# Where ring pieces and moving tiles start within 64 bytes of SBUF: a two-block transformer kernel on one core

## The reference, cut to what matters

```python
h  = modulate(rmsnorm(x)) ; parts = h @ w_in          # first block: gated linear attention, Fourier mix
y  = (gate_fft * (fft @ w_fourier_out) + gate_gla * (o @ w_gla_out)) @ w_out
x  = x + gt1 * y
x  = x + gt2 * (square(relu(h2 @ w_mlp_in)) @ w_mlp_out)   # 2048 -> 8192 -> 2048
u  = rms_norm(x) @ w_in_2                              # second block: 2048 -> 4352
y  = concat(mixers(u)) @ w_out_2                       # 2048 -> 2048
up = rms_norm(x) @ w_up_2                              # 2048 -> 11264, then conv and gate
x  = x + rms_norm((silu(gate) * val) @ w_down_2)       # 5632 -> 2048
```

## Time and profile before

| | us |
|---|---|
| median of 3 runs | 2663.68 (2663.1 to 2665.05) |
| the profiled execution, its own time | 2666.81 |
| its span, first to last instruction | 2665.0 |
| TensorE busy in the span | 2587.0 |
| ScalarE, VectorE busy | 1139.6, 1658.2 |
| mean granted TensorE clock | 0.986 |

### The profile page before, as it was taken

The page is one execution under the profiler, slowest core; times in us unless marked ns, Lnnn a source line. Parts: engine busy times, 40 slices in busy tenths (PEclk is TensorE's granted clock), DMA queues, the critical chain, the costliest instruction groups (busy, mean ns, idle before and its releaser), DMA issues.

```text
span 2665.0 us, 42761 instructions
## 1 busy us (share of the span) xinstructions
PE 2587.0 (97%) x19024; PEld 2417.4 (91%) x19024; DVE 1658.2 (62%) x1989; ACT 1139.6 (43%) x1293; POOL 11.2 (0%) x24
## 2 busy tenths in 40 slices
PE   6799999999998999999999999999899999999998
PEld 4478799789997999999999999899899889988996
DVE  4266566557786754555555568966667647764775
ACT  3332555534435443434434454044445435543544
POOL 0000000000000000000000000000000000000000
PEclk9899999999998999999999999999999999999999
DMA  9776555567875765555555555445355555555553
GB/s 373 303 265 238 193 202 206 175 219 283 300 292 186 285 208 188 190 188 182 186 188 190 176 178 200 145 158 189 131 190 181 199 188 190 179 201 190 190 178 121
DMA packets 77225, 547.77 MB, mean 206 GB/s; under 512 B 8849, under 2 KB 8977, under 8 KB 12273
## 3 DMA queue, kind: packets, MB, share of 16 engines
q1 hardware_dynamic: 74304, 533.53, 56.9%
q0 software_dynamic: 2448, 11.01, 1.1%
q10 hardware_dynamic: 288, 0.50, 0.1%
HBM read 539.77 MB, written 5.24 MB: 205 GB/s over the span
## 4 chain that ended last, share of the span: by engine, by line
PE 92%; DMA 3%; DVE 3%; ACT 2%; issue 1%; SPq 0%; POOL 0%; DVEq 0%; ACTq 0%
PE acc L286 22%; PE acc L284 22%; PE acc L288 22%; PE acc L304 5%; PE acc L305 5%; PE acc L306 5%; PE acc L341 4%; DMA raw<-in_w_mod 2%; PE mp L304 1%; PE mp L306 1%; PE mp L305 1%; PE mp L371 1%; DVE macc L415 1%; PE mp L1820 1%; DVE wlo L252 0%
## 5 line engine op out<-in xcount | busy, mean ns | idle before, releaser
L252 DVE TENSOR_TENSOR wlo<-raw,whi 128x1024 fp32r<-128x1024 f32 x781 | 945.1, 1223 | 733.4 <-ACT whi L242 730.8
L242 ACT ACTIVATE whi<-raw 128x1024 fp32r<-128x1024 f32 x781 | 819.8, 1058 | 1220.5 <-PE acc L288 906.0
L284 PE MATMUL acc<-hh,whi 128*128 128x256 f32 x3360 | 946.9, 282 | 13.5 <-DVE wlo L252 7.8
L286 PE MATMUL acc<-hl,whi 128*128 128x256 f32 x3360 | 939.1, 279 | 0.0
L288 PE MATMUL acc<-hh,wlo 128*128 128x256 f32 x3360 | 935.6, 278 | 0.0
L284 PEld LDWEIGHTS acc<-hh,whi 128*128 128x128 f32 x3360 | 633.1, 188 | 19.9 <-issue 13.4
L286 PEld LDWEIGHTS acc<-hl,whi 128*128 128x128 f32 x3360 | 634.6, 189 | 1.4 <-issue 1.0
L288 PEld LDWEIGHTS acc<-hh,wlo 128*128 128x128 f32 x3360 | 631.9, 188 | 0.0
L286 PE MATMUL acc<-ml,whi 128*128 128x256 f32 x1536 | 431.1, 281 | 0.0
L284 PE MATMUL acc<-mh,whi 128*128 128x256 f32 x1536 | 428.3, 279 | 1.6 <-DVE wlo L252 1.6
L288 PE MATMUL acc<-mh,wlo 128*128 128x256 f32 x1536 | 427.0, 278 | 0.0
(11 more groups left out here) (310 smaller groups left out, 2219.0 us busy)
## 6 DMA issues: line engine op xcount, KB each, us to landing
raw<-in_w_in SPq DMA_DIRECT2D x98, 1024.0 KB, 4.9
raw<-in_w_mod SPq DMA_DIRECT2D x96, 1024.0 KB, 5.4
raw<-in_w_up SPq DMA_DIRECT2D x88, 1024.0 KB, 4.9
raw<-in_w_mlp_in SPq DMA_DIRECT2D x64, 1024.0 KB, 4.9
raw<-in_w_mlp_out SPq DMA_DIRECT2D x64, 1024.0 KB, 4.9
raw<-in_w_down SPq DMA_DIRECT2D x44, 1024.0 KB, 4.9
raw<-in_w_out SPq DMA_DIRECT2D x32, 1024.0 KB, 5.0
raw<-in_w_fourier_out SPq DMA_DIRECT2D x8, 1024.0 KB, 5.2
```

Of the source, the lines that this page charges most:

```text
L242: nc.scalar.activation(whi[:, r, :], raw_slot(k)[:, 2 * GC * j:2 * GC * (j + 1)], ACT.Copy)\
L252: nc.vector.tensor_tensor(wlo[:, r, :], raw_slot(k)[:, 2 * GC * j:2 * GC * (j + 1)], whi[:, r, :].bitcast(f32), ALU.subtract).then_inc(S[" ...
L284: nc.tensor.matmul(dst, whi[:, r, cols], hi[:, kt, :], start=begin, stop=False, skip_group_check=True)
L286: nc.tensor.matmul(dst, whi[:, r, cols], lo[:, kt, :], start=False, stop=False, skip_group_check=True)
```

## The change: what it does

Each ring slot grows from 1024 to 1040 elements (4096 to 4160 bytes), and a table PLACE says for each piece how many elements behind its slot's start it begins: 0, 4 or 8, which is offset 0, 16 or 32. All users go through a new function `ring`.

- 332 pieces (w_mlp_in, w_mlp_out, w_in_2, w_out_2) go from offset 16 to 32.
- The 88 pieces of w_down_2 go from 16 to 0.
- All others stay at 16.
- The activation tiles of the MLP, w_in_2 and w_out_2 get new tensors over the same regions, 16 bytes further: `nh`/`nl` in place of `hh`/`hl`, `rh`/`rl` in place of `mh`/`ml`. Their offset goes from 32 to 48. The merge in front of w_out keeps `mh`/`ml`, and w_up_2 keeps `hh`/`hl`.
- The two rings are 192 bytes longer each and the region of `hh` 64 bytes. What lies behind moves by 192, 384 or 448 bytes, all multiples of 64.

No instruction is added, removed or reordered; no size, wait or queue changes.

```diff
+BLOCK = len(PIECE) - 588
+PLACE = [4] * len(PIECE)
+PLACE[BLOCK:BLOCK + 332] = [8] * 332
+for _end, _n in ((len(PIECE) - 168, 32), (len(PIECE) - 72, 32), (len(PIECE), 24)):
+    PLACE[_end - _n:_end] = [0] * _n
...
-        whi = sb("whi", [P, 8 * GC + 16], f32r)[:, 4:8 * GC + 4].rearrange("p (r n) -> p r n", r=4)
-        wlo = sb("wlo", [P, 8 * GC + 16], f32r)[:, 4:8 * GC + 4].rearrange("p (r n) -> p r n", r=4)
+        whi = sb("whi", [P, 4, 2 * GC + 16], f32r)
+        wlo = sb("wlo", [P, 4, 2 * GC + 16], f32r)
...
-        (hh, hl, xN, gN) = overlay(
-            "region_h", 32768,
+        (hh, hl, nhl, xN, gN) = overlay(
+            "region_h", 32768 + 64,
             [("hh", [P, KT, NT], f32r), ("hl", [P, KT, NT], f32r)],
+            [("nhl", [P, 2 * KT * NT + 16], f32r)],
...
+            [("rhl", [P, 2 * KT * NT + 16], f32r)],
...
+        halves = lambda ap: [ap[:, 4 + i * KT * NT:4 + (i + 1) * KT * NT].rearrange("p (k n) -> p k n", n=NT)
+                             for i in range(2)]
+        (nh, nl), (rh, rl) = halves(nhl), halves(rhl)
...
+        def ring(part, p):
+
+            return part[:, p % 4, PLACE[p]:PLACE[p] + 2 * GC]
...
-            nc.scalar.activation(whi[:, r, :], raw_slot(k)[:, 2 * GC * j:2 * GC * (j + 1)], ACT.Copy)\
+            nc.scalar.activation(ring(whi, st.p), raw_slot(k)[:, 2 * GC * j:2 * GC * (j + 1)], ACT.Copy)\
...
             for c in range(0, MLP_CHUNKS):
                 for g in range(4):
-                    mm_feature(pe, st, g % 2, hh, hl, 0, each=n2_ready if c + g == 0 else None,
+                    mm_feature(pe, st, g % 2, nh, nl, 0, each=n2_ready if c + g == 0 else None,
...
-                    mm_feature(pe, st, g % 2, mh, ml, 1, free=(S["rsq_ok"], 4 * c + g + 3) if g < 2 else None,
+                    mm_feature(pe, st, g % 2, rh, rl, 1, free=(S["rsq_ok"], 4 * c + g + 3) if g < 2 else None,
```

More of the change, by code:

```diff
@@ L249, in lo_piece @@
                 mod_acc(dve, st)
-            r = st.p % 4
             dve.wait_ge(S["hi_n"], st.p + 1)
-            nc.vector.tensor_tensor(wlo[:, r, :], raw_slot(k)[:, 2 * GC * j:2 * GC * (j + 1)],
-                                    whi[:, r, :].bitcast(f32), ALU.subtract).then_inc(S["lo_n"], 1)
+            nc.vector.tensor_tensor(ring(wlo, st.p), raw_slot(k)[:, 2 * GC * j:2 * GC * (j + 1)],
+                                    ring(whi, st.p).bitcast(f32), ALU.subtract).then_inc(S["lo_n"], 1)
             st.p += 1
@@ L274, in feature_piece @@
         def feature_piece(pe, st, i, hi, lo, k0, nkt=KT, w=GC):
-            r = st.p % 4
+            wh, wl = ring(whi, st.p), ring(wlo, st.p)
             pe.wait_ge(S["lo_n"], st.p + 1)
@@ L283, in feature_piece @@
                     begin = kt == 0 and t % 2 == 0
-                    nc.tensor.matmul(dst, whi[:, r, cols], hi[:, kt, :], start=begin, stop=False,
+                    nc.tensor.matmul(dst, wh[:, cols], hi[:, kt, :], start=begin, stop=False,
                                      skip_group_check=True)
-                    nc.tensor.matmul(dst, whi[:, r, cols], lo[:, kt, :], start=False, stop=False,
+                    nc.tensor.matmul(dst, wh[:, cols], lo[:, kt, :], start=False, stop=False,
                                      skip_group_check=True)
-                    last = nc.tensor.matmul(dst, wlo[:, r, cols], hi[:, kt, :], start=False,
+                    last = nc.tensor.matmul(dst, wl[:, cols], hi[:, kt, :], start=False,
                                             stop=kt == nkt - 1, skip_group_check=True)
@@ L303, in token_piece @@
                     dst = bank[:, off:off + GC]
-                    nc.tensor.matmul(dst, hi[:, kt, t0:t0 + P], whi[:, r, cols], start=kt == 0, stop=False)
-                    nc.tensor.matmul(dst, hi[:, kt, t0:t0 + P], wlo[:, r, cols], start=False, stop=False)
-                    last = nc.tensor.matmul(dst, lo[:, kt, t0:t0 + P], whi[:, r, cols], start=False,
+                    nc.tensor.matmul(dst, hi[:, kt, t0:t0 + P], wh[:, cols], start=kt == 0, stop=False)
+                    nc.tensor.matmul(dst, hi[:, kt, t0:t0 + P], wl[:, cols], start=False, stop=False)
+                    last = nc.tensor.matmul(dst, lo[:, kt, t0:t0 + P], wh[:, cols], start=False,
                                             stop=kt == nkt - 1)
@@ L355, in mm_lr @@
                     dst = acc[i][0:LRW, x * GC:x * GC + NT]
-                    nc.tensor.matmul(dst, whi[:, r, cols], hi[:, kt, :], start=kt == 0, stop=False)
-                    nc.tensor.matmul(dst, whi[:, r, cols], lo[:, kt, :], start=False, stop=False)
-                    last = nc.tensor.matmul(dst, wlo[:, r, cols], hi[:, kt, :], start=False, stop=kt == KT - 1)
+                    nc.tensor.matmul(dst, wh[:, cols], hi[:, kt, :], start=kt == 0, stop=False)
+                    nc.tensor.matmul(dst, wh[:, cols], lo[:, kt, :], start=False, stop=False)
+                    last = nc.tensor.matmul(dst, wl[:, cols], hi[:, kt, :], start=False, stop=kt == KT - 1)
             last.then_inc(S["used"], 1)
@@ L1278, in _ @@
             own(nc.vector.reciprocal(rstd[:, 0, :], root[:, :]))
-            apply_dve(dve, 8, 0, [(xT2, hh, hl, a, n) for a, n in N2_JOBS])
+            apply_dve(dve, 8, 0, [(xT2, nh, nl, a, n) for a, n in N2_JOBS])
             def mix_lo(g):
@@ L1909, in mixer_sums @@
                     last.then_inc(S["ln_ps"], 1)
[L1910 to L1912 removed]
+            mm_feature(pe, st, 0, nh, nl, 1, each=mixer_sums)
+            mm_feature(pe, st, 1, nh, nl, 1)
+            mm_feature(pe, st, 0, nh, nl, 1, w=NT)
             def mixed(s):
```

31 lines of the change are left out of this document (15 added, 16 removed).

## The result

The changed kernel is slower: 2681.8 us (median of 4, 2678.9 to 2684.4) against 2664.4, a ratio of 1.0060 with a 95% interval of 1.0046 to 1.0074. Forecast were 2646 us and 0.993; the time also lies above the range's end of 2672.

The account below looks back on a forecast made before the run. TensorE's matmul pitch was taken to set the time. Gains of 17 + 2 = 19 us took the profiled execution from 2666.8 to 2648 us; from the runs' median of 2663.7 the forecast was 2646, range 2618 to 2672.

Parts of the forecast that it names:

- Slots of 4160 bytes: Fifth step: longer slots and new places modulo 128 and more touch every piece, w_up_2 too; nothing in the sum.
- rival "the slots": Residues beyond 64 bytes slow w_up_2 by 9 us and the first block by 5; 2678 us, chance 0.08.
- slow gait: The slower of two steady pitches at equal offsets, 117.8 against 115.6 ns; the MLP runs in it from 880 us.
- first step: MLP, w_in_2 and w_out_2 at 32/48: about 320 pieces go from 117.8 to 115.6 ns, 17 us gained; chance 0.46.
- Second step: w_down_2's 88 pieces at offset 0: 2 us gained, bounds 17 us gained and 4 us lost.
- Third and fourth: ScalarE's and VectorE's accesses at new offsets cost the same, and DMA stays hidden at share 0.56; no time change.
- The bound of 108 ns: Least pitch taken for float32r matmuls of 256 columns, from plain float32's 216 ns; at most 78 us gained.
- quicker than any row: Rival: the new offsets give 111.8 ns a matmul and w_down_2 gains too, 57 us in all; 2607 us, chance 0.13.
- a third of the way, 2625: Milder case of "quicker than any row": the time if only a third of the pitch above 108 ns goes.
- nothing moves: Rival: only the ring-to-tile distance, 16 bytes before and after, decides; w_down_2 brings 2 us at most; 2662 us, chance 0.24.
- Off the grid: Rival: moving tiles at 48, off multiples of 32 bytes, cost 4.4 ns a matmul; 26 us more, 2690 us, chance 0.09.
- The rule of 16-byte lines: SBUF reads cost more only when leaving a 16-byte line after fewer than two hits; so nothing changes, 2663.7 us.

Follow-up runs that it names:

- e1_slots: Kernel before with only the ring slots changed, from 4096 to 4160 bytes, offsets modulo 64 kept: 2685.9 us, ratio 1.0081.
- e3_dist: Kernel before with `wlo` 16384 in place of 16448 bytes behind `whi`, all else at its address: 2690.1 us, ratio 1.0092.
- e2_dense32: Changed kernel with slots of 4096 bytes again and every ring piece at offset 32: 2678.7 us, ratio 1.0055.
- nudge8: Kernel before with eight plain float32 matmuls of 256 columns added at the start of the MLP's second chunk: 2666.8 us, ratio 1.0013.

## Why the prediction was wrong, step by step

- **The step that failed is the fifth, "Slots of 4160 bytes".** It put nothing in the sum, "as the slots before lay at equal residues and each stage was steady over all four slots". Equal residues were the reason to expect a difference, not to expect none. e1_slots shows the cost: 22 us (1.0081). By pitch w_up_2 is 168 x 24 x 3.2 ns = 12.9 of it and the first block 144 x 24 x 2.4 = 8.3, of which the profiled execution's length shows 1.5; the MLP is 4.6. The rival "the slots" had the mechanism, at a chance of 0.08, and priced it too low, at 9 and 5 us with nothing for the MLP, because it took the slow gait for the worst: the slots at 119.8 lie above it. What I held against it, that 64 bytes between `whi` and `wlo` "exist now and show nothing", was empty: a constant can't show its effect, and the change made that distance 0 modulo 256, unseen. e3_dist shows what it is worth: w_up_2 goes from 115.6 to 120.0 ns, most of the MLP from 117.8 to 120.0.
- **The first step, the quick gait for the MLP, did not come.** At 32/48 the MLP has 118.3 and 118.5 ns with slots of 4096, 118.3 on the mean with the new ones; the term of 17 us gained was really about 4 us lost in the changed kernel (3.2 and 0.4 by the table). The argument that a new setting is more likely to leave the slow gait than to fall below it took 117.9 for a ceiling. Runs at other places reached 120.0.
- **What the first step said of gaits is right in part.** A gait keeps itself up and is taken up at re-entry: one plain matmul moves 216 pieces from 117.78 to 115.56 ns, 216 x 24 x 2.2 = 11.5 us. But the offsets don't choose between the two gaits of the old places; other places have other gaits. That it is a relation in time between the two reads of TensorE is not shown by any run.
- **Second step, w_down_2:** 2 us forecast, 232.6 to 231.1 ns measured, 1056 x 1.5 = 1.6 us. Right in size. The slots alone don't bring it (e1_slots has 232.5), but with them the four slots differ (228.3 to 232.9), so what the offset 0 gives by itself is not shown. The other bound was slightly off: 232.4 and twice 2.2 ns is 236.8 and 4.6 us, not 236 and 4.
- **Third and fourth, conversions and DMA hidden:** right, 1223 and 1057 ns, DMA share 0.54, no new wait.
- **The bound of 108 ns** was half of plain float32's 216, read as one matmul. nudge8 shows that 216 ns is one of the two records of such a matmul. No stage of any run came below 115.5, and the rival "quicker than any row" fails with it. Its "a third of the way, 2625" doesn't follow either: a third of 7.6 ns below 115.6, and of the 17 us, is 2620.
- **The rival "nothing moves"** fails by e2_dense32. **"Off the grid"** (2690, the moving stream off 32 bytes) lies near in time but by another cause: w_up_2, whose tiles never left the grid, pays most. Its 4.4 ns are not there; 32/48 costs 0.5 to 0.7.
- **The rule of 16-byte lines** (the Trainium skill, page "SBUF — State Buffer", section "Door 1: The DMA port swizzle") would have all these kernels at one pitch. The runs have every operand at a multiple of 16 and contiguous, and go from 115.6 to 120.0 ns. The measurement decides: the rule says nothing of two streams read at once. The 109.2 ns that the prediction sets beside it is by the Trainium skill, page "TensorE: Matmul & The Clock Gate", section "Back-to-back issue gap", the gap of a single matmul by itself, not of a stream of weight loads and matmuls.

## What to carry to other kernels

When TensorE streams weights and moving tiles from SBUF without pause, their places modulo 256 bytes are a tuning parameter, worth up to 4% of the pitch here (115.6 to 120.0 ns), and a change of stride or of a tensor's size moves it for every stage that uses the ring, also for those that the edit means to leave alone. A ring's stride that is a multiple of 256 bytes gave all slots of a stage one pitch, but not a good one by itself: e3_dist had such a stride and the slowest w_up_2 of all runs. So write down the distances modulo 256 between hi ring, lo ring and moving tile before and after an edit, and choose places by measured pitch, stage by stage. Read the pitch as matmuls per window: the mean duration of a matmul's record hides it, and if one stage shows two pitches at the same addresses, try a single extra matmul at a point of entry before touching any layout.

## What the runs showed of the hardware

- Pitch of float32r matmuls of 256 columns at the 2.4 GHz level, ring at 16 and moving tile at 32 modulo 64, slots of 4096 bytes, by the places modulo 256 (columns: moving tile minus `whi`; rows: `wlo` minus `whi`); two numbers are two gaits, each seen to last over whole stages:

| | 16 | 80 | 144 | 208 |
|---|---|---|---|---|
| 64 | 115.6, 117.8 | 117.15 | 117.8, 120.0 | 117.8 |
| 0 | 117.2, 120.0 | | | |
| 128 | 117.8, 118.5 | 118.5 | | |
| 192 | 117.8 | 117.8 to 118.6 | | |

- The same two distances with ring at 32 and moving tile at 48 modulo 64 (e2_dense32, `nh`) have 118.3 ns, so the table holds for its own offsets alone. In all of its runs `whi` itself begins at 144 modulo 256.
- With 512 columns a stage's pitch goes from 228.9 (rings 128 apart) to 233.3 ns (0 apart) in w_down_2.
- A plain float32 matmul of 256 columns stands as two records of 216 ns each, 0.43 us: the eight of nudge8 are "x16" in its timeline, and with the re-entry behind them they took 3.5 us.
- The mechanism below the residues, which reads of the two streams meet and what a meeting costs, is not shown by these runs. The three streams of ScalarE, VectorE and the DMA write and read beside them in all of the kernels alike, and no run took them away.
